# Expert lists of 96 places in up to three passes, in place of 128 places in up to two

## The chip, the cores and the metric

The kernel runs on one core of a Trainium2 chip. The metric is the device time in microseconds (us) of one execution; smaller is better. "The kernel before" holds lists of 128 places, "the changed kernel" lists of 96.

## What is computed

A decoder trunk of two layers on 256 tokens of width 1024, float32. Nearly two thirds of the time goes to its last part, the mixture of experts, which is all that the change touches:

```python
def swiglu(h, w_gate, w_up, w_down):
    return (jax.nn.silu(h @ w_gate) * (h @ w_up)) @ w_down
...
    logits = (t @ w_router).astype(jnp.float32)
    top_vals, top_idx = lax.top_k(logits, TOP_K)
...
    for e in range(N_EXPERTS):
        out = out + swiglu(t, w_gate[e], w_up[e], w_down[e]) * gates[:, e:e + 1]
```

There are 8 experts with a hidden width of 3584, and each token goes to 2 of them (`TOP_K`). So 512 pairs of token and expert are spread over 8 lists, 64 on average. Worked out from the reference with its inputs, the eight lists hold 75, 54, 77, 75, 57, 43, 87 and 44 tokens.

## The kernel before

Each engine has its own program, and they meet at semaphores. The weights, 1 MB a "unit", stream through a ring of seven slots (`raw`, loads issued by SyncE). ScalarE casts each unit to `w_hi` (L714), VectorE computes the rest `w_lo` = raw - w_hi (L1015), both in rings of three slots, and TensorE multiplies both by the activations, split in the same way: `product` makes three matmuls of 512 moving columns for each 128 rows of weights (L1469 to L1471). The moving operand is the weight, the stationary one the activations, whose columns are the tokens.

The part with experts works on items. An item is one expert and one list of up to P = 128 of its tokens. The number of trips of the item loop is read from `trips`: 7 if no expert has more than 128 tokens, 15 if one has (a second pass over all eight experts), and one last item, written out behind the loop, follows. Before the loop VectorE makes the tables of routing (L1347 to L1358) and TensorE gathers the tokens of the first list by matmuls with a 0/1 matrix `e_choose` (L1737). In the loop POOL fetches the rows of the next list by an indirect DMA (L689).

An item has 7 steps (`STEPS`) of 6 units. In a step TensorE does: the gate product of the next 512 hidden columns (24 matmuls), four transposes of the hidden block `e_hid` (L1502; `turn`), the up product (24), the down product of the block before (24). ScalarE takes silu (L956) and copies the turned block to `eT_hi` (L976); VectorE multiplies (L1337) and makes `eT_lo` (L1379). Step 5 also has two small matmuls that sum the columns of the next list (L1768, four records in the trace), and step 6 turns the fetched rows with eight transposes (`turn_rows`), which L950 and L1331 copy to `xe_hi` and `xe_lo`. The last item adds the other experts' results from DRAM to `x_sb` (L1404) in steps 3 to 6 and goes on with the final norm.

A transpose is a matmul whose stationary operand is the data (128 columns) and whose moving operand is the identity:

```python
            def turn(key, src, n):
                dst = ready(key)
                for m in range(n):
                    mm = nc.tensor.transpose(dst[:, m * P:(m + 1) * P], src[:, m * P:(m + 1) * P], c_("ident"))
                group(mm, *key)
```

Of the kernel before, what the change touches and what calls it, by code (L numbers as in the profile page):

```python
# [24 lines left out]
P = 128  # L25
# [6 lines left out]
F_DENSE, F_EXPERT, N_EXPERTS = 2816, 3584, 8  # L32
NORM_EPS, SUBLN_EPS = 1e-6, 1e-5
# [380 lines left out]
def stream(nc, ins, out, table):  # L414
# [17 lines left out]
    with ExitStack() as ctx:  # L432
# [112 lines left out]
        e_choose, e_sil, e_hid = area(4096, TILES, P), area(4352, BLK), area(4864, BLK)  # L545
        e_route, e_cur, e_weight = area(5376, 8, 2 * N_EXPERTS), area(5504, 8), area(5512, 1)
# [5 lines left out]
        os_hi, os_lo = actB_hi[:, BLK:BLK + D], actB_lo[:, BLK:BLK + D]  # L552
        slots = actB_hi[:, BLK + D:BLK + D + SEQ]
# [22 lines left out]
        def _(sp):  # L576
# [44 lines left out]
            trip = sp.value_load(trips[0:1, 0:1], min_val=N_EXPERTS - 1, max_val=2 * N_EXPERTS - 1)  # L621
# [15 lines left out]
        def _(pool):  # L637
# [46 lines left out]
            trip = pool.value_load(trips[0:1, 0:1], min_val=N_EXPERTS - 1, max_val=2 * N_EXPERTS - 1)  # L684
            with pool.Fori(0, trip) as i:
# [3 lines left out]
                pool.indirect_dma_start(e_in, None, h_dram[:, :], bass.IndirectOffsetOnAxis(ap=token_at[:, 0:1], axis=0)  # L689
# [3 lines left out]
                pool.indirect_dma_start(y_dram[:, :], bass.IndirectOffsetOnAxis(ap=y_at[:, 0:1], axis=0), e_out, None  # L693
# [9 lines left out]
        def _(act):  # L703
# [243 lines left out]
            def gathered(key, count):  # L947
                for g in range(2):
                    act.wait_ge(sem["pe_done"], w.pe(*key, g))
                    nc.scalar.copy(xe_hi[:, g * BLK:(g + 1) * BLK], bank((*key, g))).then_inc(sem["xe_hi"], 1)  # L950

            def silu(key, s):
# [3 lines left out]
                nc.scalar.activation(e_sil, bank(key), ACT.Silu).then_inc(sem["e_sil"], 1)  # L956
# [8 lines left out]
            trip = act.value_load(trips[0:1, 0:1], min_val=N_EXPERTS - 1, max_val=2 * N_EXPERTS - 1)  # L965

            def item(at, last):
                used, end = first_loop_unit, first_loop_unit + ITEM_UNITS - (4 if last else 0)
                limit = end if last else end + AHEAD
                for s in range(1, STEPS + 1):  # L970
# [5 lines left out]
                    nc.scalar.copy(eT_hi, bank((at, "e_turn", s - 1))).then_inc(sem["e_turn_hi"], 1)  # L976
# [3 lines left out]
                    if s == 2 and last:  # L980
                        act.wait_ge(sem["pe_done"], w.pe(at, "slots_turn"))
                        nc.scalar.copy(slots, bank((at, "slots_turn"))[:, 0:SEQ]).then_inc(sem["slots_turn"], 1)
# [893 lines left out]
```

## Time and profile before

| what | value |
|---|---|
| median of 3 runs | 1530.63 us (1530.01 to 1531.14) |
| time of the profiled execution | 1530.5 us |
| its span, first to last instruction | 1528.6 us |
| mean granted clock of TensorE | 0.989 of full speed (2.4 GHz) |
| the part with experts (gather to end) | 555.6 to 1528.6 us |

The profiled execution's own time lies 1.9 us above its span and 0.1 us below the median. In the profile PE is TensorE's matmuls, PEld its loads of the stationary operand, DVE VectorE, ACT ScalarE, POOL GpSimd. Matmuls are pipelined: the pace is the distance of two starts, not the duration of one.

### The profile page before, as it was taken

To read this page: it belongs to the slowest core of one execution; us is meant where nothing else is said; L and a number is where in the kernel's file an instruction comes from. 1 tells how busy PE (TensorE), PEld (TensorE's weight loads), DVE (VectorE), ACT (ScalarE), POOL (GpSimd) and SP (SyncE) were. 2 spreads that over 40 slices of the span, in tenths; PEclk is the share of its full clock that TensorE was granted. 3 is DMA by queue.
4 is the path that set the end of the run, shared out by engine and by line. 5 is a ranking of instruction groups with operands and counts; after the bars stand their busy time and mean duration, and the time that the engine had idled before them with its cause. 6 is when DMAs were issued, how large, how long until landed. Compare 5 with 4: busy or idle time off the path is not lost.

```text
span 1528.6 us, 18741 instructions
## 1 busy us (share of the span) xinstructions
PE 1484.9 (97%) x6848; PEld 1228.0 (80%) x6848; DVE 1181.0 (77%) x946; ACT 972.4 (64%) x829; POOL 43.0 (3%) x43
## 2 busy tenths in 40 slices
PE   8999999999999789999999999999999999999996
PEld 6878788888787678888888888888888888888885
DVE  6464455555597558888888888888898888888896
ACT  5444454334446457777777777777777777777774
POOL 1000000000000000000000000000000000000000
PEclk9999999999999889999999999999999999999999
DMA  9744545554452139999999999999999999999991
GB/s 380 281 166 151 172 164 205 183 187 164 145 213 111 60 133 371 364 379 384 373 391 380 369 378 387 376 381 378 384 375 372 379 386 367 390 363 380 423 388 79
DMA packets 64877, 455.25 MB, mean 298 GB/s; under 512 B 7201, under 2 KB 7329, under 8 KB 11457
## 3 DMA queue, kind: packets, MB, share of 16 engines
q1 hardware_dynamic: 61344, 440.85, 75.6%
q0 software_dynamic: 3488, 13.80, 2.3%
q8 instruction: 29, 0.48, 0.1%
q14 instruction: 16, 0.12, 0.0%
HBM read 446.76 MB, written 7.86 MB: 297 GB/s over the span
## 4 chain that ended last, share of the span: by engine, by line
PE 90%; DVE 5%; ACT 3%; issue 2%; DMA 0%; DVEq 0%; SPq 0%; POOLq 0%; POOL 0%; ACTq 0%
PE psum L1469 28%; PE psum L1471 28%; PE psum L1470 28%; PE psum L1502 3%; DVE w_lo L1015 2%; ACT w_hi L714 1%; DVE soft L1199 0%; PE psum L1523 0%; PE psum L1737 0%; PE psum L1715 0%; DVE x_sb L1050 0%; DVE work L1214 0%; PE psum L1515 0%; ACT work L855 0%; DVE psum L1198 0%
## 5 line engine op out<-in xcount | busy, mean ns | idle before, releaser
L1015 DVE TENSOR_TENSOR w_lo<-raw,w_hi 128x2048 fp32r<-128x2048 f32 (+1 forms) x420 | 948.8, 2274 | 244.0 <-ACT w_hi L714 240.8
L714 ACT CAST w_hi<-raw 128x2048 fp32r<-128x2048 f32 (+1 forms) x420 | 799.6, 1904 | 321.6 <-PE psum L1471 320.4
L1469 PE MATMUL psum<-w_hi,actA_hi 128*128 128x512 f32 (+1 forms) x1376 | 542.9, 395 | 4.3 <-DVE actA_lo L1254 2.3
L1471 PE MATMUL psum<-w_hi,actA_lo 128*128 128x512 f32 (+1 forms) x1376 | 534.7, 389 | 0.0
L1470 PE MATMUL psum<-w_lo,actA_hi 128*128 128x512 f32 (+1 forms) x1376 | 534.1, 388 | 0.0
L1469 PEld LDWEIGHTS psum<-w_hi,actA_hi 128*128 128x128 f32 x1376 | 259.7, 189 | 57.9 <-DVE w_lo L1015 3.1
L1471 PEld LDWEIGHTS psum<-w_hi,actA_lo 128*128 128x128 f32 x1376 | 259.3, 188 | 54.3
L1470 PEld LDWEIGHTS psum<-w_lo,actA_hi 128*128 128x128 f32 x1376 | 259.8, 189 | 50.6 <-issue 0.5
L1469 PE MATMUL psum<-w_hi,actB_hi 128*128 128x512 f32 x632 | 247.9, 392 | 4.9 <-DVE actB_lo L1379 1.5
L1471 PE MATMUL psum<-w_hi,actB_lo 128*128 128x512 f32 x632 | 246.1, 389 | 0.0
L1470 PE MATMUL psum<-w_lo,actB_hi 128*128 128x512 f32 x632 | 245.9, 389 | 0.0
L1469 PEld LDWEIGHTS psum<-w_hi,actB_hi 128*128 128x128 f32 x632 | 118.6, 188 | 30.4 <-issue 3.6
L1471 PEld LDWEIGHTS psum<-w_hi,actB_lo 128*128 128x128 f32 x632 | 118.7, 188 | 24.9
L1470 PEld LDWEIGHTS psum<-w_lo,actB_hi 128*128 128x128 f32 x632 | 118.7, 188 | 24.3 <-issue 0.2
L956 ACT ACTIVATE work<-psum 128x512 f32<-128x512 f32 x56 | 33.5, 599 | 49.0 <-PE psum L1471 49.0
L1502 PEld LDWEIGHTS psum<-const,work 128*128 128x128 f32 x420 | 51.2, 141 | 12.6 <-issue 1.7
L1502 PE MATMUL psum<-const,work 128*128 128x128 f32 x420 | 60.2, 275 | 1.1 <-ACT work L786 0.8
L1379 DVE TENSOR_TENSOR actB_lo<-psum,actB_hi 128x512 fp32r<-128x512 f32 x56 | 38.3, 683 | 1.0 <-ACT actB_hi L976 1.0
L1337 DVE TENSOR_TENSOR work<-work,psum 128x512 f32<-128x512 f32 x56 | 38.1, 680 | 0.0
L976 ACT CAST actB_hi<-psum 128x512 fp32r<-128x512 f32 x56 | 32.6, 583 | 1.2 <-PE psum L1502 1.2
L689 POOL DMA_INDIRECT work<-h_dram,token_at x7 | 15.5, 2221 | 584.7 <-DVE token_at L1398 584.7
L1050 DVE TENSOR_TENSOR x_sb<-x_sb,psum 128x512 f32<-128x512 f32 x32 | 21.4, 683 | 8.5 <-PE psum L1471 8.4
(159 smaller groups left out, 472.5 us busy)
## 6 DMA issues: line engine op xcount, KB each, us to landing
raw<-in_moe_w_gate SPq DMA_DIRECT2D x112, 1024.0 KB, 7.2
raw<-in_moe_w_up SPq DMA_DIRECT2D x112, 1024.0 KB, 7.4
raw<-in_moe_w_down SPq DMA_DIRECT2D x112, 1024.0 KB, 7.0
raw<-in_ret_w_in SPq DMA_DIRECT2D x22, 1024.0 KB, 13.4
raw<-in_ffn_w_gate SPq DMA_DIRECT2D x11, 1024.0 KB, 4.8
raw<-in_ffn_w_up SPq DMA_DIRECT2D x11, 1024.0 KB, 4.8
raw<-in_ffn_w_down SPq DMA_DIRECT2D x10, 1024.0 KB, 4.8
raw<-in_ret_w_out SPq DMA_DIRECT2D x8, 1024.0 KB, 4.7
```

The lines of the kernel that those rows point to most:

```text
L689: pool.indirect_dma_start(e_in, None, h_dram[:, :], bass.IndirectOffsetOnAxis(ap=token_at[:, 0:1], axis=0)).then_inc(sem["rows_in"], 16)
L714: nc.scalar.copy(w_hi[:, u % SPLIT_SLOTS, 0:size], raw[:, u % RAW_SLOTS, 0:size]).then_inc(sem["hi_ready"], 1)
L956: nc.scalar.activation(e_sil, bank(key), ACT.Silu).then_inc(sem["e_sil"], 1)
L976: nc.scalar.copy(eT_hi, bank((at, "e_turn", s - 1))).then_inc(sem["e_turn_hi"], 1)
L1015: nc.vector.tensor_tensor(w_lo[:, slot, 0:size], raw[:, u % RAW_SLOTS, 0:size], as_f32(w_hi[:, slot, 0:size]), ALU.subtract).then_inc(sem[ ...
L1050: nc.vector.tensor_tensor(v, v, bank(key), ALU.add).then_inc(sem["x_sum"], 1)
L1337: nc.vector.tensor_tensor(e_hid, e_sil, bank(key), ALU.mult).then_inc(sem["e_hid"], 1)
L1379: nc.vector.tensor_tensor(eT_lo, bank((at, "e_turn", s - 1)), as_f32(eT_hi), ALU.subtract).then_inc(sem["e_turn_lo"], 1)
L1469: nc.tensor.matmul(dst, l_hi[:, k, cols], r_hi[:, kk, rcols], start=first, stop=False)
L1470: nc.tensor.matmul(dst, l_hi[:, k, cols], r_lo[:, kk, rcols], start=False, stop=False)
L1471: return nc.tensor.matmul(dst, l_lo[:, k, cols], r_hi[:, kk, rcols], start=False, stop=last)
L1502: mm = nc.tensor.transpose(dst[:, m * P:(m + 1) * P], src[:, m * P:(m + 1) * P], c_("ident"))
```

## The change

`LIST` = 96 takes the place of `P` wherever a list is meant, and `PASSES` = 3 the place of two halves. An expert's list now holds up to 96 tokens; a second pass over all experts is made if one has more than 96 tokens, a third if one has more than 192. Matmuls of the products have a stationary operand of 96 columns, transposes a moving one of 96, copies of turned blocks are 384 elements wide in place of 512, and elementwise work on a list takes 96 partitions. The table of routing gets a third part. The core of the diff:

```diff
+LIST = 96
+PASSES = -(-SEQ // LIST)
...
-        e_choose, e_sil, e_hid = area(4096, TILES, P), area(4352, BLK), area(4864, BLK)
...
+        e_choose, e_sil, e_hid = area(4096, TILES, LIST), area(4352, BLK)[0:LIST], area(4864, BLK)[0:LIST]
...
-        e_in, e_out, y_back = area(2048, D), area(3072, D), area(6144, TILES, 2, D)
+        e_in, e_out, y_back = area(2048, D)[0:LIST], area(3072, D)[0:LIST], area(6144, TILES, 2, D)
...
-        xe_hi, xe_lo = actA_hi[:, 0:D], actA_lo[:, 0:D]
-        eT_hi, eT_lo = actB_hi[:, 0:BLK], actB_lo[:, 0:BLK]
...
+        xe_hi, xe_lo = actA_hi[:, 0:KC * LIST], actA_lo[:, 0:KC * LIST]
+        eT_hi, eT_lo = actB_hi[:, 0:4 * LIST], actB_lo[:, 0:4 * LIST]
...
-                pool.indirect_dma_start(e_in, None, h_dram[:, :], bass.IndirectOffsetOnAxis(ap=token_at[:, 0:1], axis=0)
+                pool.indirect_dma_start(e_in, None, h_dram[:, :], bass.IndirectOffsetOnAxis(ap=token_at[0:LIST, 0:1], axis=0)
...
-                nc.scalar.activation(e_sil, bank(key), ACT.Silu).then_inc(sem["e_sil"], 1)
+                nc.scalar.activation(e_sil, bank(key)[0:LIST], ACT.Silu).then_inc(sem["e_sil"], 1)
...
-                    nc.scalar.copy(eT_hi, bank((at, "e_turn", s - 1))).then_inc(sem["e_turn_hi"], 1)
+                    nc.scalar.copy(eT_hi, bank((at, "e_turn", s - 1))[:, 0:4 * LIST]).then_inc(sem["e_turn_hi"], 1)
...
-                    nc.vector.tensor_scalar(e_choose[:, t, :], c_("iota"), e_cur[:, t:t + 1], None, ALU.is_equal
+                    nc.vector.tensor_scalar(e_choose[:, t, :], c_("iota", 0, LIST), e_cur[:, t:t + 1], None, ALU.is_equal
...
-                    part = (slice(None), slice(g * BLK, (g + 1) * BLK))
-                    nc.vector.tensor_tensor(xe_lo[part], bank((*key, g)), as_f32(xe_hi[part]), ALU.subtract
+                    part = (slice(None), slice(g * 4 * LIST, (g + 1) * 4 * LIST))
+                    nc.vector.tensor_tensor(xe_lo[part], bank((*key, g))[:, 0:4 * LIST], as_f32(xe_hi[part]), ALU.subtract
...
-                nc.vector.tensor_tensor(e_hid, e_sil, bank(key), ALU.mult).then_inc(sem["e_hid"], 1)
+                nc.vector.tensor_tensor(e_hid, e_sil, bank(key)[0:LIST], ALU.mult).then_inc(sem["e_hid"], 1)
...
-            step(nc.vector.tensor_scalar(top[:, 125:126], busiest, float(P), float(N_EXPERTS), ALU.is_gt, ALU.mult))
-            step(nc.vector.tensor_scalar(e_route[:, 0:2, N_EXPERTS:], place, -1.0 - P, None, ALU.add))
-            nc.vector.tensor_scalar(trips[:, :], top[:, 125:126], float(N_EXPERTS - 1), None, ALU.add
+            for n in range(1, PASSES):
+                step(nc.vector.tensor_scalar(top[:, 124 + n:125 + n], busiest, float(n * LIST), float(N_EXPERTS), ALU.is_gt, ALU.mult))
+            for n in range(1, PASSES):
+                step(nc.vector.tensor_scalar(e_route[:, 0:2, n * N_EXPERTS:(n + 1) * N_EXPERTS], place, -1.0 - n * LIST, None, ALU.add))
+            nc.vector.scalar_tensor_tensor(trips[:, :], top[:, 125:126], float(N_EXPERTS - 1), top[:, 126:127], ALU.add, ALU.add
...
-            for half in range(2):
+            for half in range(PASSES):
...
-                    nc.vector.tensor_tensor(eT_lo, bank((at, "e_turn", s - 1)), as_f32(eT_hi), ALU.subtract
+                    nc.vector.tensor_tensor(eT_lo, bank((at, "e_turn", s - 1))[:, 0:4 * LIST], as_f32(eT_hi), ALU.subtract
...
-                            mm = nc.tensor.matmul(dst[:, k * P:(k + 1) * P], h_rows[:, t, (4 * g + k) * P:(4 * g + k + 1) * P],
+                            mm = nc.tensor.matmul(dst[:, k * LIST:(k + 1) * LIST], h_rows[:, t, (4 * g + k) * P:(4 * g + k + 1) * P],
...
-            xe = (chunks(xe_hi, P), chunks(xe_lo, P))
-            eT = (chunks(eT_hi, P), chunks(eT_lo, P))
-            every = slice(0, P)
+            xe = (chunks(xe_hi, LIST), chunks(xe_lo, LIST))
+            eT = (chunks(eT_hi, LIST), chunks(eT_lo, LIST))
+            every = slice(0, LIST)
...
-                        mm = product(dst, xe, 4 * half + kk, every, right, kk, slice(0, BLK), half == kk == 0, half == 1 and kk == 3)
+                        mm = product(dst[0:LIST], xe, 4 * half + kk, every, right, kk, slice(0, BLK), half == kk == 0, half == 1 and kk == 3)
...
-                    mm = nc.tensor.matmul(dst[:, 0:3], e_choose[:, t, :], e_cur[:, 2 + 3 * t:5 + 3 * t],
+                    mm = nc.tensor.matmul(dst[0:LIST, 0:3], e_choose[:, t, :], e_cur[:, 2 + 3 * t:5 + 3 * t],
...
+            def turn_list(key, src):
+                dst = ready(key)
+                for m in range(4):
+                    mm = nc.tensor.transpose(dst[:, m * LIST:(m + 1) * LIST], src[:, m * P:(m + 1) * P], c_("ident")[0:LIST, 0:LIST])
...
-                    turn((*key, g), e_in[:, g * BLK:(g + 1) * BLK], 4)
+                    turn_list((*key, g), e_in[:, g * BLK:(g + 1) * BLK])
...
-                    turn((at, "e_turn", s - 1), e_hid, 4)
+                    turn_list((at, "e_turn", s - 1), e_hid)
...
-                                mm = product(bank(key), eT, 2 * half + kk, every, right, kk, slice(c * BLK, (c + 1) * BLK),
+                                mm = product(bank(key)[0:LIST], eT, 2 * half + kk, every, right, kk, slice(c * BLK, (c + 1) * BLK),
```

TensorE's program, at the transposes of a step in the item loop, before (`work` is the hidden block, `const` the identity; line numbers of each kernel are its own):

```order
L1469 MATMUL psum<-w_hi,actA_hi 128x512
L1470 MATMUL psum<-w_lo,actA_hi 128x512
L1471 MATMUL psum<-w_hi,actA_lo 128x512
L1502 MATMUL psum<-const,work 128x128 x4
L1461 REGISTER_ALU
L1469 MATMUL psum<-w_hi,actA_hi 128x512
```

The same place in the changed kernel:

```order
L1473 MATMUL psum<-w_hi,actA_hi 96x512
L1474 MATMUL psum<-w_lo,actA_hi 96x512
L1475 MATMUL psum<-w_hi,actA_lo 96x512
L1779 MATMUL psum<-const,work 128x96 x4
L1465 REGISTER_ALU
L1473 MATMUL psum<-w_hi,actA_hi 96x512
```

Nothing moved: the numbers of matmuls and of transposes are the same. A product's result has 96 partitions and the same 512 columns, and a transpose's has 96 columns.

VectorE's program ahead of the loop, from the fullest list to the first `xe_lo`, before (`top` and `work` hold the tables):

```order
L1347 TENSOR_REDUCE top<-psum 128x1
L1349 TENSOR_SCALAR top<-top 128x1
L1350 TENSOR_SCALAR work<-top 128x2x8
L1351 TENSOR_SCALAR trips<-top 128x1
L1355 COPY work<-top 128x2x8
L1357 TENSOR_SCALAR work<-top,const 128x8
...
L1358 TENSOR_SCALAR work<-top,const 128x8
L1315 COPY work<-work 128x6
L1015 TENSOR_TENSOR w_lo<-raw,w_hi 128x2048
L1331 TENSOR_TENSOR actA_lo<-psum,actA_hi 128x512 x2
```

The same place in the changed kernel:

```order
L1349 TENSOR_REDUCE top<-psum 128x1
L1352 TENSOR_SCALAR top<-top 128x1 x2
L1354 TENSOR_SCALAR work<-top 128x2x8 x2
L1355 SCALAR_TENSOR_TENSOR trips<-top 128x1
L1359 COPY work<-top 128x2x8
L1361 TENSOR_SCALAR work<-top,const 128x8
...
L1362 TENSOR_SCALAR work<-top,const 128x8
L1317 COPY work<-work 128x6
L1017 TENSOR_TENSOR w_lo<-raw,w_hi 128x2048
L1333 TENSOR_TENSOR actA_lo<-psum,actA_hi 128x384 x2
```

Two instructions are added ahead of `trips` and a block of five (one copy, four TENSOR_SCALAR) behind it, all in front of the `w_lo` and the `xe_lo` (`actA_lo`) that follow.

## Rows read from the trace of the kernel before

**Rows 1.** The page: the span, and ScalarE's cast of the weights.

```profile
span 1528.6 us, 18741 instructions
...
L714 ACT CAST w_hi<-raw 128x2048 fp32r<-128x2048 f32 (+1 forms) x420 | 799.6, 1904 | 321.6 <-PE psum L1471 320.4
```

**Rows 2.** Waits from 600 to 1480 us: who waited for whom, us, times, longest.

```profile
PE psum L1469 <- DVE w_lo L1015: 0.2, 1, 0.2
```

**Rows 3.** Busy us of the engines, clock, DMA share and GB/s in stretches.

```profile
1000.00:1100.00 100.00, 100.00 (x460) 82.89 (x460) 88.33 (x53) 75.55 (x52) 3.20 (x2) 1.00 0.99 383
...
1450.00:1460.00 10.00, 9.84 (x44) 7.83 (x43) 10.00 (x7) 6.33 (x5) 0.00 (x0) 1.00 1.01 420
```

**Rows 4.** The chain that ended last: the eight transposes of step 6 in two items.

```profile
668.59 0.87 PE psum L1502 x8
...
1382.67 0.87 PE psum L1502 x8
```

**Rows 5.** Timeline around one step's four transposes: start, us, engine, line.

```profile
1019.33 0.39 PE L1471 MATMUL psum<-w_hi,actA_lo 128*128 128x512 f32 x1
...
1019.56 0.60 PE L1502 MATMUL psum<-const,work 128*128 128x128 f32 x4
...
1019.88 0.19 PEld L1469 LDWEIGHTS psum<-w_hi,actA_hi 128*128 128x128 f32 x1
...
1020.23 0.40 PE L1470 MATMUL psum<-w_lo,actA_hi 128*128 128x512 f32 x1
```

**Rows 6.** TensorE's timeline in step 5: transposes, column sums, products.

```profile
1002.32 0.60 PE L1502 MATMUL psum<-const,work 128*128 128x128 f32 x4
1002.76 0.51 PE L1768 MATMUL psum<-work 128*128 128x3 f32 x4
...
1003.44 0.40 PE L1470 MATMUL psum<-w_lo,actA_hi 128*128 128x512 f32 x1
```

**Rows 7.** TensorE's timeline, matmuls of 256 columns: first and last of 45.

```profile
372.65 0.28 PE L1469 MATMUL psum<-w_hi,actA_hi 128*128 128x256 f32 x1
...
377.93 0.28 PE L1471 MATMUL psum<-w_hi,actA_lo 128*128 128x256 f32 x1
```

**Rows 8.** Instructions of two lines: duration ns min/median/max, first and last start.

```profile
L1502 PEld LDWEIGHTS psum<-const,work x268: 138/139/141, 611.4 to 1497.3; 128*128 128x128 f32 x134
L1502 PE MATMUL psum<-const,work x268: 270/272/273, 611.7 to 1497.4; 128*128 128x128 f32 x134
...
L1768 PEld LDWEIGHTS psum<-work x32: 187/192/192, 566.4 to 1360.0; 128*128 128x128 f32 x32
```

**Rows 9.** Timeline, transposes that follow idle time: two matmuls, two loads.

```profile
125.66 0.41 PE L1502 MATMUL psum<-const,work 128*128 128x128 f32 x2 [0.47 <-ACT work L786]
...
125.63 0.20 PEld L1502 LDWEIGHTS psum<-const,work 128*128 128x128 f32 x2 [0.68 <-issue]
```

**Rows 10.** Timeline ahead of the loop: VectorE's tables and first `xe_lo`, TensorE's gather.

```profile
556.07 0.17 DVE L1355 COPY work<-top 128x16 f32<-128x16 f32 x1
...
556.94 0.17 DVE L1355 COPY work<-top 128x16 f32<-128x16 f32 x1
...
560.10 0.68 DVE L1331 TENSOR_TENSOR actA_lo<-psum,actA_hi 128x512 fp32r<-128x512 f32 x1
...
555.60 5.75 PE L1737 MATMUL psum<-work 128*128 128x128 f32 x32 [1.32 <-issue]
561.10 0.48 PE L1469 MATMUL psum<-w_hi,actA_hi 128*128 128x512 f32 x1
```

**Rows 11.** The page: the two copies of a turned block.

```profile
L1379 DVE TENSOR_TENSOR actB_lo<-psum,actB_hi 128x512 fp32r<-128x512 f32 x56 | 38.3, 683 | 1.0 <-ACT actB_hi L976 1.0
...
L976 ACT CAST actB_hi<-psum 128x512 fp32r<-128x512 f32 x56 | 32.6, 583 | 1.2 <-PE psum L1502 1.2
```

**Rows 12.** TensorE's timeline in the last item: the transposes of steps 3 and 4.

```profile
1444.98 0.60 PE L1502 MATMUL psum<-const,work 128*128 128x128 f32 x4
...
1462.23 0.60 PE L1502 MATMUL psum<-const,work 128*128 128x128 f32 x4
```

More of the change, by code:

```diff
@@ L620, in _ @@
             sp.wait_ge(sem["routed"], 1)
-            trip = sp.value_load(trips[0:1, 0:1], min_val=N_EXPERTS - 1, max_val=2 * N_EXPERTS - 1)
+            trip = sp.value_load(trips[0:1, 0:1], min_val=N_EXPERTS - 1, max_val=PASSES * N_EXPERTS - 1)
             with sp.Fori(0, trip) as i:
@@ L683, in _ @@
             pool.wait_ge(sem["routed"], 1)
-            trip = pool.value_load(trips[0:1, 0:1], min_val=N_EXPERTS - 1, max_val=2 * N_EXPERTS - 1)
+            trip = pool.value_load(trips[0:1, 0:1], min_val=N_EXPERTS - 1, max_val=PASSES * N_EXPERTS - 1)
             with pool.Fori(0, trip) as i:
@@ L949, in gathered @@
                     act.wait_ge(sem["pe_done"], w.pe(*key, g))
-                    nc.scalar.copy(xe_hi[:, g * BLK:(g + 1) * BLK], bank((*key, g))).then_inc(sem["xe_hi"], 1)
+                    nc.scalar.copy(xe_hi[:, g * 4 * LIST:(g + 1) * 4 * LIST], bank((*key, g))[:, 0:4 * LIST]).then_inc(sem["xe_hi"], 1)
             def silu(key, s):
@@ L964, in _ @@
             act.wait_ge(sem["routed"], 1)
-            trip = act.value_load(trips[0:1, 0:1], min_val=N_EXPERTS - 1, max_val=2 * N_EXPERTS - 1)
+            trip = act.value_load(trips[0:1, 0:1], min_val=N_EXPERTS - 1, max_val=PASSES * N_EXPERTS - 1)
             def item(at, last):
@@ L1368, in _ @@
             dve.wait_ge(sem["routed"], 1)
-            trip = dve.value_load(trips[0:1, 0:1], min_val=N_EXPERTS - 1, max_val=2 * N_EXPERTS - 1)
+            trip = dve.value_load(trips[0:1, 0:1], min_val=N_EXPERTS - 1, max_val=PASSES * N_EXPERTS - 1)
             def item(at, i, last):
@@ L1385, in item @@
                         slot_sums = bank(("slots",))
-                        nc.vector.tensor_copy(e_weight, slot_sums[:, 0:1]).then_inc(sem["slots_read"], 1)
-                        nc.vector.tensor_scalar(y_at[:, :], slot_sums[:, 1:2], c_("token", 0, 1), None, ALU.max
+                        nc.vector.tensor_copy(e_weight, slot_sums[0:LIST, 0:1]).then_inc(sem["slots_read"], 1)
+                        nc.vector.tensor_scalar(y_at[0:LIST, :], slot_sums[0:LIST, 1:2], c_("token", 0, 1)[0:LIST], None, ALU.max
                                                 ).then_inc(sem["slots_read"], 1)
@@ L1767, in slot_sums @@
                 for t in range(TILES):
-                    mm = nc.tensor.matmul(dst[:, 0:3], e_choose[:, t, :], e_cur[:, 2 + 3 * t:5 + 3 * t],
+                    mm = nc.tensor.matmul(dst[0:LIST, 0:3], e_choose[:, t, :], e_cur[:, 2 + 3 * t:5 + 3 * t],
                                           start=t == 0, stop=t == TILES - 1)
+                group(mm, *key)
+            def turn_list(key, src):
+                dst = ready(key)
+                for m in range(4):
+                    mm = nc.tensor.transpose(dst[:, m * LIST:(m + 1) * LIST], src[:, m * P:(m + 1) * P], c_("ident")[0:LIST, 0:LIST])
                 group(mm, *key)
@@ L1783, in _ @@
             pe.wait_ge(sem["routed"], 1)
-            trip = pe.value_load(trips[0:1, 0:1], min_val=N_EXPERTS - 1, max_val=2 * N_EXPERTS - 1)
+            trip = pe.value_load(trips[0:1, 0:1], min_val=N_EXPERTS - 1, max_val=PASSES * N_EXPERTS - 1)
             loop_start = list(count)
@@ L1800, in item @@
                         for t in range(TILES):
-                            mm = nc.tensor.transpose(dst[:, tokens(t)], e_choose[:, t, :], c_("ident"))
+                            mm = nc.tensor.transpose(dst[0:LIST, tokens(t)], e_choose[:, t, :], c_("ident"))
                         group(mm, at, "slots_turn")
```

16 lines of the change are left out of this document (8 added, 8 removed).

## Prediction

> **What bounds the kernel now.** I looked at the waits first, then at stretches of 100 us, then at the pace of single instructions. From 600 to 1480 us TensorE waited 0.2 us for anything at all [rows 2], and in a stretch of the item loop it is busy throughout at full clock while VectorE has 12% of its time left [rows 3]. ScalarE's cast waits for TensorE to free a slot in 320.4 of its 321.6 idle us, never for a transfer [rows 1]. DMA's share of 0.99 looks like a bound and isn't one: the loads are issued when a slot comes free, at 383 GB/s, and another stretch moves 420 [rows 3]. So the loop goes at TensorE's pace, and a us taken from TensorE there is a us of the kernel until another engine runs out of slack.
>
> The loop's period is (1382.67 - 668.59) / 6 = 119.01 us an item [rows 4]. Of what is it made? From 1003.44 to 1019.33 lie 70 matmuls of 512 columns, 227.0 ns each [rows 5, 6]. Those of 256 columns stand (377.93 - 372.65) / 44 = 120.0 ns apart [rows 7]. The difference is 107 ns for 256 columns, one column per period of 2.4 GHz, and the rest is a fixed 13.3 ns at either width. An item's 504 product matmuls are 114.4 us; the other 4.6 us are 36 transposes and the four records of the column sums.
>
> **Which width sets the time of a product.** The change narrows the stationary operand (the tokens), from 128 columns to 96, and leaves the moving one at 512. TensorE's streaming time follows the moving width by the two paces above. The load of the next stationary operand lies under it: exposed, a load costs about 0.11 us (below), half of a matmul of 512. So 96 columns in place of 128 leave 4032 matmuls (8 items of 504) at 227 ns, and a quarter less arithmetic gives nothing there. Not shown by any row is whether the fixed 13.3 ns (32 periods) depends on the stationary width, since every matmul of this trace has 128. I take it as fixed; the bounds are with the rivals.
>
> **The transposes** are another case: here the moving operand is the identity, and it goes from 128 to 96 columns, while the stationary one (the data) keeps 128. Four of them start at 1019.56, and the product behind them effectively starts at 1020.23 - 0.227 = 1020.00 [rows 5]: 0.44 us for four, 0.11 each. Either the moving side sets this (two periods a column, 107 ns) or the load of 128 columns does (107 ns as well). The rows favour the moving side. Loads of a transpose last 139 ns, those of plain fp32 192 ns [rows 8], 53 ns more, which is half of 107. Behind idle time a transpose's load starts at 125.63; the second transpose starts at 125.66 + 0.41 - 0.272 = 125.80 [rows 8, 9], so the first began to stream at about 125.69, 0.06 us after its load started. A product's exposed load takes 1020.00 - 1019.88 = 0.12 us from start to streaming [rows 5]. A transpose's load is thus the shorter one, about 0.055 us, and hides under even 80 ns of streaming. At 96 columns I expect 80 ns a transpose, 26.7 ns less. The load of the product behind the group (now 96 columns) shrinks from 107 to 80 ns and stays hidden under the last transpose.
>
> - Plain groups of four: 4 x 26.7 = 0.107 us; six an item: 0.64.
> - The eight transposes of step 6: 0.21.
> - Step 5, transposes and column sums: 1003.44 - 0.227 - 1002.32 = 0.89 us for eight [rows 6]; the four column sums stream three columns, so their loads of `e_choose` set the pace, at 0.11 each. Those loads narrow to 96 columns: 8 x 26.7 = 0.21.
>
> Together 1.07 us an item, 7.5 us in seven trips. For the loads of 96 columns the estimate is 96/128 of the 107 ns.
>
> The Trainium skill ("TensorE: Matmul & The Clock Gate", section LDWEIGHTS) gives a load as columns / 1.2 in ns, whatever the number of rows. The exposed loads of products agree with its 107 ns for 128 columns; the transposes' 0.06 us does not, and by the rule the transposes would keep their pace, which is the first rival below.
>
> **VectorE and ScalarE in the loop.** L976 and L1379 narrow to 384 elements, at most a quarter of 583 and 683 ns [rows 11]; I take 0.1 and 0.13 us. Both lie under TensorE's products, as does the shorter gather of rows by POOL. They cost or give nothing there, but they keep the slack that TensorE's 0.11 us a step takes away. Nothing new waits, and loads would come at 383 x 119.01 / 117.94 = 386 GB/s, under the 420.
>
> **Ahead of the loop, a cost.** VectorE gets seven more small instructions in front of `xe_lo`. A block of five takes 556.94 - 556.07 = 0.87 us [rows 10], so seven about 1.2. The first `xe_lo` then starts at 561.3 in place of 560.10 [rows 10] and ends, narrower, near 561.9. TensorE now begins its first product at 561.10, straight behind the gather [rows 10]. It will wait 0.8 us; everything behind it starts that much later. The gather itself may get shorter by at most a quarter of 5.75 us [rows 10], which that wait would swallow.
>
> **The last item and the end.** Steps 3 and 4 are 17.25 us apart [rows 12] where the loop has (119.01 - 0.87 - 0.45) / 7 = 16.81 (less the eight transposes and the column sums): VectorE, with the addition to `x_sb` on top, is late there with `w_lo`. In these four steps the transposes' gain is eaten by a longer wait, and what counts is that L976 lets ScalarE's next cast start 0.1 us earlier: 0.4. The other three steps give 0.107 each, 0.3. In step 7 L976 and L1379 lie in series in front of the last down product: 0.23. Sum 0.95. The first list's column sums give 0.13.
>
> **Sum:** -7.5 - 0.95 - 0.13 + 0.8 = -7.8 us. Against the profiled execution's 1530.5 us, which is 0.1 below the median, that is 1522.7, and I say **1522.8 us**, 0.5% less. Its own range, from the waits and widths that I rounded, is 1521 to 1525.
>
> **Does it do what it says?** The gate of more than 96 tokens must stay shut. The fullest list has 87, so `trips` stays 7. Were one list over 96, eight more items of 119.01 would come: 1530 + 952 = 2480 us. Chance 1%; it would take other inputs.
>
> **Rivals.**
> 1. *The transposes keep their 107 ns*, because a load of 128 columns sets it after all, or because a transpose's moving side is not charged by columns. For it: the two times coincide at 128; against it: 139 against 192 ns, and the 0.06 us. Then only the column sums' loads gain, 4 x 26.7 = 0.107 us an item, 0.9 us in all; with the last item 0.4 + 0.23 less and 0.8 more, -0.7: 1529.8 us. Chance 16%. The Trainium skill's rule named above is the one that speaks for it.
> 2. *The fixed 13.3 ns follow the stationary width* (32 periods for 128 columns, 24 for 96). For it: the odd number; against it: it is the same at 256 and 512 moving columns, which says nothing of the other side. 4032 x 3.3 ns = 13.4 us more gain: 1509.4 us. Chance 10%.
> 3. *Slower: a product with 96 stationary columns goes at a worse pace.* Its place is every product of the loop. It decides at 10.9 us (7.8 + 3.1), so from 2.7 ns a matmul. No row has such an operand; the bound is 13.3 ns the other way, and an equal step of 3.3 ns up would give 1536.2 us. Chance 6%.
>
> The Trainium skill (same page, section on weight-path modes) says that fast weight load needs exactly 128 weights and a type other than FP32. If the products had it, the change would lose it. Here product loads last as long as the plain fp32 ones, and take 0.12 us exposed, so the trace shows no fast load to lose.
>
> **How the numbers follow.** My forecast has 67%, the rivals 16, 10 and 6, the extra pass 1. 0.2% (3.1 us) is about what a measurement can tell from no change. Faster: 67 + 10 = 77%, less a little for a forecast that several small misses could spoil: 0.74. Same: 16% and those misses, 0.18. Slower: 0.08. The range must reach rival 1 and leaves out 2, 3 and the extra pass: 1519 to 1531.
>
> **What would show it.** An item's period of 117.94 us; product pace 227 ns; four transposes in 0.34 us, eight in 0.66; TensorE busy throughout in the loop; its first product near 561.9; the last item's steps 3 to 6 near 17.15. A period of 118.9 is rival 1, 116.3 rival 2, above 119 rival 3. I would be wrong most likely about the transposes, whose pace carries 6 of the 7.8 us.

## The result, and the profile after

The changed kernel takes **1539.74 us** (median of four runs, 1539.60 to 1539.94) where the kernel before took 1530.76 (four runs). The ratio is 1.0059, with a 95% interval of 1.0047 to 1.0071: 0.6% slower, outside the predicted range and on the side that had 8 chances in 100. The profiled execution is one of the four, 1539.6 us.

The page of the kernel after, its span and the rows that answer to [rows 1]; TensorE's product loads now have 96 columns:

```profile
span 1537.8 us, 18748 instructions
...
L716 ACT CAST w_hi<-raw 128x2048 fp32r<-128x2048 f32 (+1 forms) x420 | 798.4, 1901 | 334.0 <-PE psum L1475 334.0
...
L1473 PEld LDWEIGHTS psum<-w_hi,actA_hi 128*96 128x96 f32 (+1 forms) x1376 | 235.6, 171 | 81.9 <-DVE actA_lo L1256 3.1
```

ScalarE's casts still wait for nothing but TensorE, 13.6 us longer for it than before. From 600 to 1480 us no wait of TensorE is left in the view of waits, and the stretch that answers to [rows 3] (busy us of PE, PEld, DVE, ACT and POOL, granted clock, DMA share, GB/s) shows TensorE just as full, at the same clock:

```profile
1000.00:1100.00 100.00, 100.00 (x457) 70.33 (x456) 86.50 (x52) 73.67 (x52) 3.10 (x2) 1.00 0.98 377
```

It has 457 records of TensorE where the same stretch had 460 before. One stretch is little to go by, since the stretches of before hold 454 to 460; the seven from 700 to 1400 us together have 3181 records after and 3211 before, 0.9% fewer. So nothing waits more, the clock is as high, memory moves less, and yet TensorE gets less done in a busy us. The chain that ended last gives the period by the groups of eight transposes (start, us), to set beside [rows 4]:

```profile
670.68 0.66 PE psum L1779 x8
...
1391.69 0.66 PE psum L1779 x8
```

(1391.69 - 670.68) / 6 = 120.17 us, against 119.01. TensorE's timeline in one item of the loop (start, us):

```profile
1019.33 0.39 PE L1475 MATMUL psum<-w_hi,actB_lo 128*96 128x512 f32 x1
...
1024.89 0.40 PE L1475 MATMUL psum<-w_hi,actA_lo 128*96 128x512 f32 x1
1025.12 0.49 PE L1779 MATMUL psum<-const,work 96*128 96x96 f32 x4
...
1025.68 0.39 PE L1474 MATMUL psum<-w_lo,actA_hi 128*96 128x512 f32 x1
```

Two things are read here. Between 1019.33 and 1024.89 lie 24 starts of products: 5.56 / 24 = **231.7 ns** each, not 227.0 [rows 5, 6]. And the four transposes take 1025.68 - 0.232 - 1025.12 = **0.33 us**, not 0.44. Both changes are in the same rows. The first counts 504 times an item, the second about ten times: six groups of four, and step 5 and step 6 with twice as much each.

The profiled executions in pieces, us (the last column is an experiment's, below; each number is a difference of starts shown here, in [rows 4], [rows 10] or below):

| piece | before | after | products at 128 again |
|---|---|---|---|
| span's start to the first product | 561.10 | 562.14 | 559.05 |
| from there to the first group of eight | 107.49 | 108.54 | 106.82 |
| six periods | 714.08 | 721.01 | 708.79 |
| from the seventh group of eight to the end | 145.93 | 146.11 | 144.84 |
| span | 1528.6 | 1537.8 | 1519.5 |

Of the 9.2 us that lie between before and after, 1.0 is the start, 8.0 the loop, 0.2 the rest. (The experiment's shorter start is not its own doing: its gather began at 552.67 us and not at 555.60, and TensorE's granted clock from 509 to 552 us, a stretch that the edit does not touch, was 0.90 in that execution and 0.86 in the other two.) The start is in TensorE's timeline:

```profile
555.75 6.60 PE L1741 MATMUL psum<-work 128*128 128x96 f32 x32 [1.28 <-issue]
562.14 0.48 PE L1473 MATMUL psum<-w_hi,actA_hi 128*96 128x512 f32 x1
```

and in VectorE's, where `xe_lo` ends at 562.09, just ahead of that product (it had started at 560.10 before, [rows 10]):

```profile
561.54 0.55 DVE L1333 TENSOR_TENSOR actA_lo<-psum,actA_hi 128x384 fp32r<-128x384 f32 x1
```

The gather took 6.60 us though it has a quarter fewer columns than the one of 5.75 us [rows 10], because of the granted clock (the third number from the right in each row below, a share of 2.4 GHz). It was 0.50 (1.2 GHz) up to the microsecond from 560 and rose in the next, while before it had risen in the one from 559. In both kernels it had stood at 0.50 since 550 us at the latest, and the engine stood still for 1.3 us ahead of the gather.

```profile
560.00:561.00 1.00, 1.00 (x7) 1.00 (x6) 1.00 (x1) 0.00 (x0) 0.00 (x0) 0.50 0.00 0
561.00:562.00 1.00, 1.00 (x8) 1.00 (x8) 1.00 (x2) 0.00 (x0) 0.00 (x0) 0.67 0.00 0
```

The rise in the kernel before:

```profile
559.00:560.00 1.00, 1.00 (x8) 1.00 (x8) 1.00 (x1) 0.58 (x1) 0.00 (x0) 0.67 0.00 0
```

### The profile page after: what moved, and what is told of

The parts are those of the page before. It is cut to its first block, busy times and chain, and to the rows that moved or that the text cites. A ratio compares the mean times of both kernels' runs of the same rounds, so it can differ in the third digit from the quotient of the medians.

```text
span 1537.8 us, 18748 instructions
## 1 busy us (share of the span) xinstructions
PE 1493.4 (97%) x6848; PEld 1115.3 (73%) x6848; DVE 1172.3 (76%) x953; ACT 963.8 (63%) x829; POOL 42.3 (3%) x43
## 4 chain that ended last, share of the span: by engine, by line
PE 92%; DVE 4%; ACT 2%; issue 1%; DMA 0%; DVEq 0%; SPq 0%; POOLq 0%; POOL 0%; ACTq 0%
PE psum L1473 29%; PE psum L1475 29%; PE psum L1474 29%; PE psum L1779 2%; DVE w_lo L1017 1%; PE psum L1506 1%; ACT w_hi L716 1%; DVE soft L1201 0%; PE psum L1527 0%; PE psum L1741 0%; PE psum L1719 0%; DVE x_sb L1052 0%; DVE work L1216 0%; DMA x_sb<-in_x 0%; ACT work L857 0%
## 5 line engine op out<-in xcount | busy, mean ns | idle before, releaser
L1473 PE MATMUL psum<-w_hi,actA_hi 128*96 128x512 f32 (+2 forms) x1376 | 544.1, 395 | 4.2 <-DVE actA_lo L1256 2.6
L1475 PE MATMUL psum<-w_hi,actA_lo 128*96 128x512 f32 (+2 forms) x1376 | 538.6, 391 | 0.0
L1474 PE MATMUL psum<-w_lo,actA_hi 128*96 128x512 f32 (+2 forms) x1376 | 536.2, 390 | 0.0
L1473 PEld LDWEIGHTS psum<-w_hi,actA_hi 128*96 128x96 f32 (+1 forms) x1376 | 235.6, 171 | 81.9 <-DVE actA_lo L1256 3.1
L1475 PEld LDWEIGHTS psum<-w_hi,actA_lo 128*96 128x96 f32 (+1 forms) x1376 | 235.3, 171 | 81.1
L1474 PEld LDWEIGHTS psum<-w_lo,actA_hi 128*96 128x96 f32 (+1 forms) x1376 | 236.2, 172 | 77.3 <-issue 0.5
L1473 PE MATMUL psum<-w_hi,actB_hi 128*96 128x512 f32 (+1 forms) x632 | 249.7, 395 | 4.7 <-DVE x_sb L1052 1.3
L1475 PE MATMUL psum<-w_hi,actB_lo 128*96 128x512 f32 (+1 forms) x632 | 248.6, 393 | 0.0
L1474 PE MATMUL psum<-w_lo,actB_hi 128*96 128x512 f32 (+1 forms) x632 | 247.4, 391 | 0.0
L1474 PEld LDWEIGHTS psum<-w_lo,actB_hi 128*96 128x96 f32 (+1 forms) x632 | 107.0, 169 | 38.5 <-issue 0.2
```

Of the source, the lines that this page charges most:

```text
L1473: nc.tensor.matmul(dst, l_hi[:, k, cols], r_hi[:, kk, rcols], start=first, stop=False)
L1474: nc.tensor.matmul(dst, l_hi[:, k, cols], r_lo[:, kk, rcols], start=False, stop=False)
L1475: return nc.tensor.matmul(dst, l_lo[:, k, cols], r_hi[:, kk, rcols], start=False, stop=last)
```

## The experiments

A mean pace of the products in the whole loop follows from each period: take off what isn't a product (4.6 us with transposes of 128 columns; 1.07 less, 3.53, with 96, as the rows of the transposes bear out) and divide by 504. Before: 227.0 ns. After: (120.17 - 3.53) / 504 = 231.4, so +4.4 ns. That is 2.2 us an item more for products and 1.07 less for transposes. It is no second proof, since the 231.4 comes out of the same period; the independent reading is the one from the timeline, 231.7 ns against 227.0. What makes up the 4.4 ns? The change gave the products' stationary operand 96 columns in place of 128, and it packed the blocks: block k starts at column 96k and not 128k.

**Products of 128 columns again, all else as changed.** The blocks lie 128 apart, ScalarE and VectorE fill the first 96 columns of each (`spread`; `packed` is the bank's first 384 columns as four blocks), and the products load all 128 (the last 32 hold what was in the buffer; their rows of the result are not read).

```diff
+        def spread(v, g=0):
+            return v[:, g * 4 * P:(g + 1) * 4 * P].rearrange("p (k n) -> p k n", k=4)[:, :, 0:LIST]
...
-                    nc.scalar.copy(xe_hi[:, g * 4 * LIST:(g + 1) * 4 * LIST], bank((*key, g))[:, 0:4 * LIST]).then_inc(sem["xe_hi"], 1)
+                    nc.scalar.copy(spread(xe_hi, g), packed(bank((*key, g)))).then_inc(sem["xe_hi"], 1)
...
-            xe = (chunks(xe_hi, LIST), chunks(xe_lo, LIST))
-            every = slice(0, LIST)
+            WIDE = 128
+            xe = (chunks(xe_hi, P), chunks(xe_lo, P))
+            every = slice(0, WIDE)
...
-                        mm = product(dst[0:LIST], xe, 4 * half + kk, every, right, kk, slice(0, BLK), half == kk == 0, half == 1 and kk == 3)
+                        mm = product(dst[0:WIDE], xe, 4 * half + kk, every, right, kk, slice(0, BLK), half == kk == 0, half == 1 and kk == 3)
```

> The changed kernel, but the products' stationary operand is 128 columns again (chunks of the turned blocks 128 apart, of which 96 are filled; the rest is old data whose results nobody reads). Lists, transposes and the third table stay at 96. Theory A (a product with 96 stationary columns goes at 231.8 ns in place of 226.7): the product pace is back at 226.7 to 227 ns, transposes stay at 0.34 us for four, period 117.9 us, about 1523.5 us. Rival B (the pace is lost to the packed layout, chunks that start at multiples of 384 bytes): also near 1523.5, told apart by the next run. Rival C (something else in the changed kernel, such as the narrower copies, slows TensorE's stream): stays near 1539.

Measured: 1524.40 us (five runs, 1521.32 to 1524.66) against 1531.01, ratio 0.9959 (0.9945 to 0.9973). Its chain and the first product, which here waited for `xe_lo`:

```profile
665.87 0.66 PE psum L1786 x8
...
1374.66 0.66 PE psum L1786 x8
```

```profile
559.05 0.50 PE L1479 MATMUL psum<-w_hi,actA_hi 128*128 128x512 f32 x1 [0.27 <-DVE actA_lo L1339]
```

The period is 118.13, the mean pace 227.4 ns. The whole loss is gone and the transposes' gain is left: the kernel is 0.4% faster than the one before and 1.0% faster than the changed one. Something else in the changed kernel (rival C) would have kept it near 1539.

**The same layout with products of 96 columns.** Only `WIDE = 96` differs from the kernel above.

> The same layout as the run before, chunks 128 apart, but the products take 96 stationary columns. Theory A: pace 231.8 ns, period 120.2 us, 1539 to 1540 us. Rival B (alignment of the chunks): pace 226.7 and about 1523.5 us. Rival C: about 1539.

Measured: 1532.98 us (ten runs) against 1531.01, ratio 1.0014 (1.0004 to 1.0023). From its groups of eight:

```profile
669.61 0.66 PE psum L1786 x8
...
1385.36 0.66 PE psum L1786 x8
```

the period is 119.29 and the mean pace 229.7 ns. The result lies between what the width alone (1539) and the packing alone (1523.5) were expected to give, so both have a part: the width is +2.7 ns over the kernel before, and the packed starts are the other 1.7.

**The kernel before, with nothing changed but the products' width.**

```diff
-            every = slice(0, P)
+            every = slice(0, 96)
...
-                        mm = product(dst, xe, 4 * half + kk, every, right, kk, slice(0, BLK), half == kk == 0, half == 1 and kk == 3)
+                        mm = product(dst[0:96], xe, 4 * half + kk, every, right, kk, slice(0, BLK), half == kk == 0, half == 1 and kk == 3)
```

(The down product likewise. The rows of places 96 to 127, which no token has, are not computed.)

> The kernel before with only the products' stationary operand and result narrowed to 96 columns; lists, transposes and tables stay at 128 (places 96 to 127 of a list are not computed, no list has that many tokens). Theory A: pace 231.8 ns, 504 x 8 x 5.1 ns = 20.6 us more than before, about 1551 us. Rivals B and C: as before, 1530.6 us.

Measured: 1540.94 us (four runs) against 1531.01, ratio 1.0067 (1.0051 to 1.0082).

```profile
670.57 0.87 PE psum L1502 x8
...
1392.53 0.87 PE psum L1502 x8
```

Period 120.33, mean pace (120.33 - 4.6) / 504 = 229.6 ns. It is 10 us less than expected, since I had put the whole excess down to the width; it confirms the split, 2.6 here and 2.7 above. Read from the starts alone, most stretches of 24 products in one item go at 226.7 ns in the kernel before, at 230.0 in this one and the one above, and at 231.7 in the changed one. By this reading the width costs 3.3 ns and the packing 1.7. The means say 0.6 ns less for the width, since they also hold what happens around the transposes, which 4.6 and 3.53 us may not catch exactly. Three lines that leave out a quarter of the loop's arithmetic cost 0.67%.

**Matmuls alone.** A kernel whose output is a copy of x, and which runs 24 matmuls of a kind in a row, first in quiet, then with ScalarE and VectorE busy.

> Matmuls alone, no work of the decoder (the output is a copy of x): runs of 24 matmuls of 512 moving columns with 128, 120, 112, 96, 96 (packed), 80, 64 and 32 stationary columns, then of 256 moving columns with 128, 96 and 64; once on a quiet core, once beside casts on ScalarE and subtractions on VectorE. Theory A1 (any width under 128 costs 5 ns): 231.8 for all but 128, and 125 in place of 120 at 256. Theory A2 (the excess grows with the missing columns): 231.8 at 96, about 234 to 237 at 64 and more at 32. Rival D (the excess comes from what else runs): 226.7 at every width in the quiet part, 231.8 only in the busy one.

Its timeline, in quiet (start, us, and the operands' shapes, stationary after the star):

```profile
22.14 5.61 PE L69 MATMUL psum<-right,left 128*128 128x512 f32 x24
27.59 5.77 PE L71 MATMUL psum<-right,left 128*120 128x512 f32 x24
33.20 5.68 PE L73 MATMUL psum<-right,left 128*112 128x512 f32 x24
38.72 5.68 PE L75 MATMUL psum<-right,left 128*96 128x512 f32 x24
44.23 5.76 PE L77 MATMUL psum<-right,left 128*96 128x512 f32 x24
...
66.53 3.03 PE L85 MATMUL psum<-right,left 128*128 128x256 f32 x24
69.39 2.94 PE L87 MATMUL psum<-right,left 128*96 128x256 f32 x24
72.17 2.88 PE L89 MATMUL psum<-right,left 128*64 128x256 f32 x24
```

The distance of two groups' starts over 24 is the pace. 128 columns: (27.59 - 22.14) / 24 = 227.1 ns. 120: 233.8. 112: 230.0. 96: 229.6; with the blocks packed 96 apart (L77): 233.3. With 256 moving columns it goes the other way, 119.2, 115.8 and 113.3 for 128, 96 and 64. The same groups beside busy ScalarE and VectorE start at the same distances (for 128, 120 and 96 columns 227.9, 233.8 and 230.0): other engines' traffic is not the cause. Neither form of theory A came out: the widths under 128 do not cost the same (A1), nor more the narrower they are (A2), and at 256 columns the sign is the other way.

**Other widths, distances and lengths, alone.**

> Matmuls alone on a quiet core (the output is a copy of x), 24 of each kind: stationary widths 128, 104, 96, 72, 48 and 16, with the start of one stationary block 128, 112, 104, 96, 64 or 0 columns behind the one before; moving widths 512, 448, 384 and 320; then transposes and plain fp32 matmuls. Theory A (the width of the stationary operand sets the excess, and a start that is no multiple of 128 columns adds to it): 227 ns for 128 wide whatever the step, 230 for 96 at steps 128 and 0, 233 for 96 at steps 96, 104 and 112. Theory B (only the start matters, the width by itself nothing): 128 wide at step 96 and 112 as slow as 96 wide, 233. For transposes, if the moving side sets their pace: 107 ns with 128 moving columns, 80 with 96, 55 to 60 with 64, whatever the stationary width; if the load does: 107 for each with 128 stationary columns, 80 with 96. Plain fp32 with 3 moving columns: 107 ns a record at 128 stationary columns, 80 at 96.

```profile
22.33 5.60 PE L60 MATMUL psum<-right,left 128*128 128x512 f32 x24
27.77 5.68 PE L62 MATMUL psum<-right,left 128*96 128x512 f32 x24
33.29 5.76 PE L64 MATMUL psum<-right,left 128*96 128x512 f32 x24
38.89 5.71 PE L66 MATMUL psum<-right,left 128*96 128x512 f32 x24
...
55.54 5.73 PE L72 MATMUL psum<-right,left 128*128 128x512 f32 x24
61.11 5.69 PE L74 MATMUL psum<-right,left 128*128 128x512 f32 x24
...
170.65 2.78 PE L118 MATMUL psum<-ident,raw 128*128 128x128 f32 x24
173.27 2.15 PE L120 MATMUL psum<-ident,raw 96*128 96x96 f32 x24
175.35 1.72 PE L122 MATMUL psum<-ident,raw 64*128 64x64 f32 x24
177.00 2.82 PE L124 MATMUL psum<-ident,raw 128*96 128x128 f32 x24
179.66 2.15 PE L126 MATMUL psum<-ident,raw 96*96 96x96 f32 x24
```

96 columns at starts 128 apart: 230.0 ns; 96 apart: 233.3. And 128 columns with starts 96 apart (L72): 232.1. So the full width isn't what protects a product: where its blocks start counts as much. Neither theory holds whole, A for this and B because 96 columns at starts 128 apart are slower than 128. In the changed kernel's loop the packed blocks went at 231.7 ns, not at the 233.3 of the same spacing here; that difference is not explained. At 448, 384 and 320 moving columns the width costs nothing more: 202.9, 174.6 and 146.7 ns for 128 columns, 202.5, 174.6 and 146.7 for 96 at starts 128 apart. The packed starts still cost something at two of them: 203.7, 176.7 and 146.7. The transposes: 109.2 ns at a moving side of 128, 86.7 at 96 (82.9 with 96 stationary columns as well), 68.8 at 64. With 96 stationary columns and a moving side of 128 (L124) it stays at 110.8: the stationary columns do not set the pace, as predicted. What does is the identity's size. Its rows shrink together with its columns, and no run here parts the two. Plain fp32 matmuls with 3 moving columns, whose loads are to set the pace, came at the end of this run, where the granted clock was 0.50 for most of them; there they took 182 and 143 ns a record for 128 and 96 stationary columns (11 and 14 records in 2 us). The expected 107 and 80 are for full clock and stay unmeasured, but the narrower load does go faster.

**One fixed block for each kind**, so that width and start stand apart.

> Matmuls of 512 moving columns alone on a quiet core (the output is a copy of x), 24 of each kind, each kind with one fixed stationary block: 96 wide with starts 0 to 128 in steps of 8 columns; widths 32 to 128 in steps of 8 from start 0; then 128 and 96 wide with the moving block's start moved by 4 to 128 columns, and 128 wide with the stationary block's start moved. Theory A1 (a number of columns short of 128 costs a fixed 3.3 ns, the start another 0 to 3.3): all 96-wide kinds between 230 and 233.3. Theory E (load and stream read the same memory and meet at times that depend on both addresses): the pace also changes with the moving block's start, for 128 wide too. If neither the moving start nor the stationary start changes 128 wide (226.7 throughout), what counted in the run before was a start that changes from one load to the next.

Pace in ns, 512 moving columns, from the distance of the groups' starts over 24; a column is 4 bytes:

| kind | start column or width | ns |
|---|---|---|
| 96 wide, stationary start | 0, 8, 16, 24, 32, 40, 48, 56 | 230.0, 229.2, 228.3, 233.7, 231.2, 231.3, 233.3, 233.3 |
| the same | 64, 72, 80, 88, 96, 104, 112, 120, 128 | 230.0, 229.2, 228.7, 230.4, 231.7, 231.2, 233.3, 233.3, 230.0 |
| width, start 0 | 32, 48, 64, 80, 88, 96, 112, 120, 128 | 231.2, 233.8, 230.0, 232.9, 227.1, 230.0, 233.3, 233.8, 227.1 |
| 128 wide, moving operand moved by | 4, 8, 16, 32, 64, 128 | 231.7, 233.3, 228.8, 232.1, 228.8, 227.5 |
| 128 wide, stationary start | 8, 16, 32, 48, 64 | 233.3, 233.3, 232.1, 229.2, 227.9 |

Three of its rows, for 120 and 128 columns and for 128 with the moving operand 4 columns on:

```profile
177.47 5.76 PE L116 MATMUL psum<-right,left 128*120 128x512 f32 x24
183.08 5.61 PE L118 MATMUL psum<-right,left 128*128 128x512 f32 x24
188.53 5.72 PE L120 MATMUL psum<-right,left 128*128 128x512 f32 x24
```

Starts 64 columns apart (256 bytes) mostly agree: 0, 64 and 128, 8 and 72, 48 and 112. Among the widths the two fast ones are 128 and 88, both from start 0. The rows for 128 columns are the cleanest: nothing but the place of one operand differs in them, and the pace goes from 227.1 to 233.3. From here on the theory (E in the expectations) is that the pace depends on where the columns streamed and the columns loaded next to each other lie in memory, and that the width is one way to change it.

**The kernel before, with its weights 32 bytes further on.** No width and no work changes. The second pad puts all tensors behind the weights, the stationary operands among them, 256 bytes further on, so "nothing else moved" below is not quite so; alone, a stationary start of 64 columns (256 bytes) had 227.9 ns against 227.1.

```diff
         raw = sb("raw", [P, RAW_SLOTS, UNIT])
+        sb("pad0", [P, 8])
         w_hi = sb("w_hi", [P, SPLIT_SLOTS, UNIT], F32R)
         w_lo = sb("w_lo", [P, SPLIT_SLOTS, UNIT], F32R)
+        sb("pad1", [P, 56])
```

> The kernel before, all widths 128, with the split weights (w_hi and w_lo, the moving operands) placed 8 columns (32 bytes) further in memory and nothing else moved. Theory E (the pace of a product depends on the addresses that its stream and the next load read): as in the runs of matmuls alone, 233.3 ns in place of 226.7 to 227.5 for products of 512 moving columns; the loop's period goes from 119.0 to about 122.2 us, and with the dense part's products of 512 (1944 of them) the time rises by up to 6000 x 6 ns = 36 us, to about 1565. Theory N (narrow stationary operands alone are slow, addresses count nothing in the real kernel): 1530.8 us, as before.

Measured: 1562.08 us (four runs, 1561.24 to 1563.23) against 1530.83, ratio **1.0208** (1.0189 to 1.0227).

```profile
681.50 0.87 PE psum L1504 x8
...
1413.18 0.87 PE psum L1504 x8
```

Period 121.95, mean pace 232.8 ns, where the kind "moved by 8" had 233.3 alone. TensorE waits for nothing here either (0.3 us of its loads from 690 to 1500). Shown: the operands' places alone change the products' pace, and by more than the whole change did.

**Lists of 88 places**, which the fullest list (87) still fits, once with products of 88 columns at starts 128 apart, and once with products of 128. The edit is `LIST = 88` in the two kernels above (`WIDE = 88` in the first).

> The changed kernel with lists of 88 places (the fullest has 87), blocks of the turned operands 128 columns apart, and products of 88 stationary columns. Theory E: a block 88 wide from an aligned start ran at 227.1 ns in the matmuls alone, where 96 wide ran at 230.0; so 504 x 2.9 ns = 1.5 us an item less than the same layout at 96 (1533.0), transposes 36 x 6.7 ns less: about 1519.5 to 1521. Theory N: narrower is no faster, 230 ns, about 1531.

> Lists of 88 places, products 128 wide, blocks 128 apart. Both theories: product pace 227 ns as in the run with 96 places (1524.4 us); transposes at 73 ns in place of 80, 36 x 8 x 6.7 ns = 1.9 us less: about 1522.5 us.

Measured: 1530.62 us for products of 88 (ten runs, 1530.07 to 1536.03; ratio 1.0009, 0.9997 to 1.0020), and 1524.06 for 128 (six runs; 0.9961, 0.9947 to 0.9976). The first misses what theory E gave (1519.5 to 1521) and lands on what theory N gave (about 1531). In an item it has both paces:

```profile
998.76 0.39 PE L1479 MATMUL psum<-w_hi,actA_hi 128*88 128x512 f32 x1
...
1003.98 0.40 PE L1481 MATMUL psum<-w_hi,actA_lo 128*88 128x512 f32 x1
...
1021.72 0.39 PE L1480 MATMUL psum<-w_lo,actA_hi 128*88 128x512 f32 x1
...
1026.80 0.39 PE L1481 MATMUL psum<-w_hi,actA_lo 128*88 128x512 f32 x1
```

(1003.98 - 998.76) / 23 = 227.0 ns, and (1026.80 - 1021.72) / 22 = 230.9; around 1033 us it is 234. So theory E, read off one fixed block, does not tell a real loop's pace at this width, and theory N's one pace of 230 ns is not what the loop has either. The second has a period of 117.90 us, 0.23 under that of lists of 96, as 36 transposes of 6.7 ns less give; in the medians, 0.34 us apart where 1.9 were expected, that can't be told from nothing.

**The third routing table alone** (the changed kernel with `LIST = 128` and `PASSES = 3`, so that all widths are those of before), and **two tables in the kernel with products of 128** (the edit below, with `trips` made by one instruction from the one gate left, as in the kernel before).

```diff
-PASSES = -(-SEQ // LIST)
+PASSES = 2
```

> The kernel before (lists of 128, all widths as before) with the third table of routing alone: seven more small VectorE instructions ahead of the first xe_lo. By the prediction's sum TensorE's first product of the experts begins 0.8 us later, about 1531.6 us against 1530.8. Rival: the gather ends later than xe_lo in most runs, since TensorE's clock is at half in it, and the cost is hidden: within 0.3 us of before.

> The run with 128-wide products again, but with two tables in place of three (seven instructions less, valid for lists of up to 192 tokens). If the third table costs what the prediction says: 0.7 us less than that run's 1524.4. If it is hidden behind the gather: the same within 0.3 us.

Measured: 1531.65 us with the third table (twelve runs, 1528.23 to 1532.77) against 1530.44, ratio 1.0005 (0.9996 to 1.0013); and 1524.59 with two tables in the kernel with products of 128 (five runs; 0.9963, 0.9951 to 0.9976), where three gave 1524.40. Neither tells the term of 0.8 us from nothing. The reason is in the timelines of the gather and the first product, here with two tables:

```profile
556.69 6.59 PE L1747 MATMUL psum<-work 128*128 128x96 f32 x32 [1.28 <-issue]
563.06 0.49 PE L1479 MATMUL psum<-w_hi,actA_hi 128*128 128x512 f32 x1
```

and with three, in the same kernel:

```profile
552.67 6.11 PE L1747 MATMUL psum<-work 128*128 128x96 f32 x32 [1.28 <-issue]
```

From the gather's start to the first product it is 563.06 - 556.69 = 6.37 us with two tables, and 559.05 - 552.67 = 6.38 with three. With two, `xe_lo` was ready at 561.74 and the product stood behind the gather, whose clock rose only in the microsecond from 562. With three, the clock rose in the microsecond from 557, 1.2 us before the gather's end, and the product waited 0.27 us for `xe_lo`. The kernel before had an early rise and no third table: 561.10 - 555.60 = 5.50 [rows 10]. By these three executions the third table costs up to 0.9 us where the clock rises early in the gather and next to nothing where it rises late; how often each happens is not known.

## Why the prediction was wrong

**The step that failed** is "Which width sets the time of a product", and in it the sentence that "96 columns in place of 128 leave 4032 matmuls (8 items of 504) at 227 ns". It put the cost of a narrower stationary operand at nothing, and no row showed that. The products went at 231.4 on the mean: 2.7 ns from the narrower operand, 1.7 from the packed blocks. That is 8 x 504 x 4.4 ns = 17.7 us, on a forecast gain of 7.8. The outcome is rival 3 in its place and its sign. Its price, "an equal step of 3.3 ns up", was too small, and I gave it 6 in 100. Its mark, a period above 119, came true.

**What misled me.** From 227.0 ns at 512 and 120.0 at 256 moving columns I read "one column per period, and a fixed 13.3 ns". Alone, 448, 384 and 320 columns go at 202.9, 174.6 and 146.7 ns. Less one period a column that leaves 16.2, 14.6 and 13.4 ns: not one constant, and two points can't tell. I also asked only what the *amount* of stationary columns does. I never asked what the change does to their *addresses*, though the diff says it plainly (`chunks(xe_hi, LIST)` for `chunks(xe_hi, P)`). All of the trace before had one width and one spacing, so it could not price either; the honest bound from the rows was wider than I made it.

**The transposes** were right: 0.33 us for four (0.34 predicted), 0.68 for eight (0.66), and step 5's eight records at 1008.66 - 0.232 - 1007.75 = 0.68 us, 0.21 less, as predicted:

```profile
1007.75 0.49 PE L1779 MATMUL psum<-const,work 96*128 96x96 f32 x4
1008.08 0.43 PE L1772 MATMUL psum<-work 128*96 128x3 f32 x4
...
1008.66 0.39 PE L1474 MATMUL psum<-w_lo,actA_hi 128*96 128x512 f32 x1
```

Rival 1 is out by these and by the transposes run alone. With 128-column products the loop and the end give 967.50 - 960.45 = 7.05 us (the three pieces ahead of the span), with a pace that is 0.4 ns worse than before in it, 4032 x 0.4 ns = 1.6 us. Without that the gain is 8.7, against the predicted 8.6 (7.5 + 0.95 + 0.13). The piece behind the seventh group alone gives 145.93 - 144.84 = 1.09, predicted 0.95. So the forecast of gains was right for a kernel that kept its products as they were. The trace also decides between the Trainium skill's rule and the row that the prediction weighed: the transposes did not keep the pace that the rule gives for their 128-column load.

**Rival 2** fell: the remainder does not follow the stationary width at 512 moving columns. At 256 it does shrink, 119.2 to 115.8 ns, 3.4 less, very near the 3.3 of that rival.

**VectorE, ScalarE, transfers.** No new wait, DMA at 377 GB/s. Right. The prediction had them lose slack; with the longer item they had more of it.

**Ahead of the loop**: `xe_lo` started at 561.54, the prediction said 561.3, and the first product at 562.14, it said 561.9. The numbers came near partly by luck: the gather, which was to end 0.8 us ahead of `xe_lo`, ran at the low clock for longer and ended with it. Whether seven instructions cost 0.8 us over many runs stays open.

**The last item.** Predicted were steps near 17.15 us and 0.95 less. Steps 3 and 4 stand 17.20 apart (17.25 before):

```profile
1454.58 0.49 PE L1779 MATMUL psum<-const,work 96*128 96x96 f32 x4
...
1471.78 0.49 PE L1779 MATMUL psum<-const,work 96*128 96x96 f32 x4
```

TensorE's slower products mostly filled waits there: the last piece of the table grew by 0.18 us only, where 504 products 4.4 ns slower would have added 2.2 us and the narrower widths taken off about 1.1. TensorE's loads waited 1.5 us for `w_lo` in this item, 2.2 before. **Trips** stayed seven.

**What stays open.** The product's pace depends on where both operands lie: shown, by moving one of them at a time in the matmuls alone, and the weights in the whole kernel. By what rule is not. The stationary start repeats only mostly in steps of 64 columns; the width's excess was seen at 512 moving columns and not at 448, 384 or 320, while the packed starts cost 2.1 ns at 384; and products of 88 columns keep 227 ns in one part of an item and not in another. That the load of the next stationary columns meets the stream at the memory is the explanation I favour, and it is argued, not shown: no run measured the memory.

## What to carry to other kernels

With 512 moving columns, narrow the moving side of a matmul, not the stationary one, unless the load is what TensorE waits for: here fewer stationary columns saved nothing and cost 0.7% by themselves, 1.0% with their blocks packed (1539.74 against 1524.40 us). When lists or blocks get shorter, keep the stationary blocks at their old starts and full width and let the spare columns run along; then the narrower transposes are pure gain (0.4% here). And when a change moves operands in memory, by packing or by a new buffer ahead of them, compare the distance between matmul starts before and after, first of all: 4 ns in 227 showed in no wait and in no busy share of TensorE's matmuls, and were the whole result.

## What was unexpected of the hardware

- Products of 512 moving columns went at 226.7 to 233.8 ns at full clock, by the operands' places and the stationary width alone. In the kernel before, moving the weights by 32 bytes (and what lies behind them by 256) cost 2.1%.
- Fewer stationary columns were no faster at 512, and mostly slower: 128 took 227.1 ns, 120 took 233.8, 32 took 231.2; only 88, at one place, took 227.1 again, and not throughout a real loop. At 256 moving columns fewer were faster.
- Transposes took about 109, 87 and 69 ns with an identity of 128, 96 and 64; 96 stationary columns for 128 changed that little (110.8 for 109.2).
